# NSA scores of query tiles 2 and 3 from high and low parts in fp32r

## The chip, the cores and the metric

The kernel runs on one NeuronCore of a Trainium2 chip. The metric is the device time of one execution in microseconds (us), the median of several runs. TensorE (PE) multiplies, VectorE (DVE) and ScalarE (ACT) work elementwise, GpSimd (POOL) works elementwise and issues indirect DMAs, SyncE (SP) issues most of the weight DMAs. PEld is TensorE's weight load.

## The reference, cut to what matters

Two transformer blocks run one after the other on 512 tokens of width 1024, in float32. The change lies in the first block, in the Native Sparse Attention (NSA): 8 heads of 64 columns in 2 key/value groups of 4 heads. It has three branches, of which two are touched, the local window of 256 tokens and the selected blocks (with top-8 of 8 blocks this is full causal attention):

```python
lg = jnp.einsum('bqghd,bgqkjd->bqghkj', q_c, k_sel).astype(jnp.float32) * scale + bias_s
p_sel = masked_softmax(lg, mask_s[:, :, :, None], (-2, -1))
o_sel = jnp.einsum('bqghkj,bgqkjd->bqghd', p_sel, v_sel.astype(jnp.float32))
...
lg = jnp.einsum('bqghd,bkgd->bqghk', q_c, kw_c).astype(jnp.float32) * scale + bias_w
p_win = masked_softmax(lg, mask_w[:, None, None, :], -1)
o_win = jnp.einsum('bqghk,bkgd->bqghd', p_win, vw_c.astype(jnp.float32))
out = g_c[..., 0:1] * o_cmp + g_c[..., 1:2] * o_sel + g_c[..., 2:3] * o_win
```

The change is about the two products of q and k (`lg`).

## The kernel before, in words

Everything is written per engine, each engine's program in its own order, joined by semaphores. Large projections are computed as three fp32r products from parts: a value is a high part (its copy rounded to fp32r) plus a low part (the value less the high part), and high x high + high x low + low x high are added up in PSUM (`products`, L2130 is its matmul helper). For each weight tile ACT makes the high part (L948), POOL the low part (L807), through two buffers `w_split`; the raw tiles come through a ring of four (`ring`, loaded by SP at L691 once POOL's low part of the tile four before is made).

`h_split`, the parts of the normed input, lies at `h_base`. It is last read by the token-major projection `vtok`, which ends right before the window attention, and is written again only in the memory attention much later.

An attention of this kernel (`attend` on PE, on DVE, and `softmax` on ACT) runs over 32 units, a unit being one head of one tile of 128 queries; 8 units for each of the query tiles t = 0 to 3. Units come in pairs: of the two heads of a pair one belongs to group 0 (partitions 0 to 63 of `qk`) and one to group 1 (partitions 64 to 127). A unit has 1, 2, 3, 3 blocks of 128 keys in the window attention (t = 0 to 3) and 1, 2, 3, 4 in the selected one. In each turn of the loop PE does, for pair n: the scores of pair n (L2230), then the product with the values of the first unit of pair n-2 (L2255), the transposes of the first unit of pair n-1 (L2245), and the same two for the second units. DVE adds the bias and takes the least (L1545) right after the scores, ACT makes the exponential (L966), PE transposes it, ACT copies the transpose out of PSUM (L983), and PE multiplies it with the values. At pair 6 of the window attention (and each fourth one after) DVE also writes out a finished query tile (L1514 to L1523; at pair 6 the gates too, L1615 to L1617).

The scores are float32 products with 64 rows of contraction. Each appears in the trace as two weight loads and two matmuls.

What stands around the window attention on POOL: the low part of the first `w_out` weight tile before pair 1 and of the second at pair 4 (L807); then nothing until 275.7 us. These two tiles are first read at 265 us, after both attentions. ACT makes their high parts at 158.7 and 165.8 us.

## Time and profile before

| | us |
|---|---|
| median of 3 runs | 2499.2 (2498.59 to 2503.46) |
| the profiled execution, its own time | 2500.74 |
| its span, first to last instruction | 2498.7 |
| PE busy | 2454.7 (98%) |
| PE weight loads busy | 2074.6 (83%) |
| DVE, POOL, ACT busy | 1578.5, 1289.3, 965.6 |
| window attention, scores of t = 2 and 3 (8 pairs) | 174.28 to 196.94 |
| selected attention, scores of t = 2 and 3 (8 pairs) | 228.90 to 253.70 |

PE is busy nearly all the time. Its matmuls are pipelined and overlap in the records (a matmul has about 0.2 us from its start to its end besides what it streams), so how fast PE works is read from the distance between the starts of instructions, not from their durations. "issue" behind an idle time says that the engine waited for nothing that the profile shows.

### The profile page before, as it was taken

The page shows a single profiled execution, that of the slowest core. Times are in us where ns is not written, and L with a number is a line of the kernel's source. Part 1 is how long each engine was busy: PE and PEld are TensorE (multiplying, and loading weights), DVE is VectorE, ACT ScalarE, POOL GpSimd, SP SyncE. Part 2 cuts the span into 40 slices and gives each one's busy share as a digit, 9 for nine tenths or more (in the row PEclk, how much of TensorE's full clock was granted, in tenths as well). Part 3 has the DMA queues.
Part 4 walks back from the last instruction along what each step waited for, and adds up shares of the span by engine and source line. Part 5 has one row for each costly group of instructions (what it writes and reads, how often), then busy time and mean ns, then how long its engine had stood idle before and what let it go on. Part 6 is the DMA issues. An engine that isn't in the chain of part 4 may idle for free.

```text
span 2498.7 us, 32840 instructions
## 1 busy us (share of the span) xinstructions
PE 2454.7 (98%) x12363; PEld 2074.6 (83%) x12363; DVE 1578.5 (63%) x2572; ACT 965.6 (39%) x1573; POOL 1289.3 (52%) x671
## 2 busy tenths in 40 slices
PE   9999999999999999999999999999999999999998
PEld 6877766877786777788789999999999888888886
DVE  2246244776402735422379897998940699999995
ACT  3256455222323435523333333434333433333333
POOL 3630322444454433144434887766666567666662
PEclk9999999999999999999999999999999999999999
DMA  5320222655433221022223888999998899999992
GB/s 215 118 68 1 68 68 76 202 197 182 152 101 127 76 85 66 32 98 93 101 81 118 297 298 287 356 354 360 358 322 260 296 363 359 364 367 361 367 363 90
DMA packets 212733, 508.90 MB, mean 204 GB/s; under 512 B 18401, under 2 KB 101345, under 8 KB 212193
## 3 DMA queue, kind: packets, MB, share of 16 engines
q1 hardware_dynamic: 123696, 338.22, 38.6%
q0 software_dynamic: 36864, 134.23, 15.1%
q10 hardware_dynamic: 52016, 34.36, 4.4%
q8 instruction: 99, 1.62, 0.3%
q14 instruction: 58, 0.47, 0.1%
HBM read 454.31 MB, written 52.43 MB: 203 GB/s over the span
## 4 chain that ended last, share of the span: by engine, by line
PE 89%; DVE 3%; POOL 3%; ACT 3%; DMA 1%; issue 1%; ACTq 0%; DVEq 0%; SPq 0%
PE bank L2130 73%; PE bank L2682 3%; PE bank_and L2130 3%; POOL weight_split L807 3%; PE bank L2255 3%; PE bank_and L2098 2%; PE bank L2245 1%; ACT weight_split L948 1%; PE bank_and L2230 1%; DMA ring<-weights 1%; PE bank L2230 1%; PE bank L2109 1%; PE bank_and L2495 0%; PE bank L2554 0%; DVE h_split L1424 0%
## 5 line engine op out<-in xcount | busy, mean ns | idle before, releaser
L2130 PE MATMUL bank<-h_split,weight_split 128*128 128x384 f32 (+1 forms) x5568 | 1133.9, 362 | 12.9 <-POOL weight_split L807 4.9
L2130 PEld LDWEIGHTS bank<-h_split,weight_split 128*128 128x128 f32 x5568 | 994.7, 188 | 126.1 <-POOL weight_split L807 11.9
L807 POOL TENSOR_TENSOR weight_split<-ring,weight_split 128x1024 fp32r<-128x1024 f32 x182 | 452.9, 2488 | 758.4 <-ACT weight_split L948 758.2
L2130 PE MATMUL bank<-late_weight_split,weighted_split 128*128 128x512 f32 x2268 | 514.8, 389 | 0.0
L2130 PEld LDWEIGHTS bank<-late_weight_split,weighted_split 128*128 128x128 f32 x2268 | 425.5, 188 | 88.3
L834 POOL DMA_INDIRECT arena<-weights,arena x256 | 314.2, 1228 | 146.1 <-DVE arena L1884 59.6
L823 POOL TENSOR_TENSOR weight_split<-ring,weight_split 128x1024 fp32r<-128x1024 f32 x129 | 310.3, 2406 | 120.8 <-ACT weight_split L1321 120.1
L948 ACT ACTIVATE weight_split<-ring 128x1024 fp32r<-128x1024 f32 x182 | 192.0, 1055 | 292.2 <-PE bank L2130 276.9
L1321 ACT ACTIVATE weight_split<-ring 128x1024 fp32r<-128x1024 f32 x130 | 137.8, 1061 | 390.2 <-PE bank L2130 336.3
L2026 DVE TENSOR_TENSOR arena<-arena 128x384 f32<-128x384 f32 x128 | 224.8, 1756 | 21.3 <-DMA arena<-expert_acts 20.9
L823 POOL TENSOR_TENSOR late_weight_split<-ring,late_weight_split 128x1024 fp32r<-128x1024 f32 x63 | 152.7, 2424 | 102.8 <-ACT late_weight_split L1321 102.2
L1884 DVE CUSTOM_DVE_ANT_0 arena<-arena,bank_and 128x1024 f32<-128x1024 f32 x128 | 153.1, 1219 | 49.6 <-DMA arena<-weights,arena 48.7
L1355 ACT ACTIVATE weighted_split<-arena 128x384 fp32r<-128x384 f32 x128 | 67.4, 527 | 270.4 <-DVE arena L2026 261.2
L2016 DVE SCALAR_TENSOR_TENSOR bank_and<-arena,bank_and 128x1024 f32<-128x1024 f32 x127 | 162.6, 1280 | 0.9
L1321 ACT ACTIVATE late_weight_split<-ring 128x1024 fp32r<-128x1024 f32 x126 | 132.8, 1054 | 46.4 <-PE bank L2130 40.5
L2130 PE MATMUL bank<-hidden_layer_split,weight_split 128*128 128x512 f32 x528 | 122.3, 392 | 1.3 <-POOL weight_split L807 1.0
L2130 PEld LDWEIGHTS bank<-hidden_layer_split,weight_split 128*128 128x128 f32 x528 | 98.3, 188 | 24.9 <-issue 2.6
L1486 DVE SCALAR_TENSOR_TENSOR arena<-bank,rstd 128x512 f32<-128x512 f32 x42 | 29.0, 691 | 126.2 <-PE bank L2130 118.0
L2032 DVE TENSOR_TENSOR weighted_split<-arena,weighted_split 128x384 fp32r<-128x384 f32 x128 | 76.2, 596 | 47.0 <-ACT weighted_split L1355 47.0
L2682 PE MATMUL bank<-arena 128*128 128x128 f32 x768 | 93.4, 275 | 0.0
L2682 PEld LDWEIGHTS bank<-arena 128*128 128x128 f32 x768 | 92.3, 192 | 0.0
L2255 PEld LDWEIGHTS bank<-arena 128*128 128x128 f32 x528 | 67.4, 191 | 24.3 <-ACT arena L983 15.8
(349 smaller groups left out, 2718.3 us busy)
## 6 DMA issues: line engine op xcount, KB each, us to landing
ring<-weights SPq DMA_DIRECT2D x493, 512.0 KB
expert_acts<-arena SPq DMA_DIRECT2D x128, 192.0 KB
gates_spread<-arena ACTq DMA_DIRECT2D x24, 1024.0 KB
arena<-gates_spread SPq DMA_DIRECT2D x96, 256.0 KB
arena<-expert_acts SPq DMA_DIRECT2D x128, 192.0 KB
arena<-weights,arena POOLq DMA_INDIRECT x256
arena<-bias_sel ACTq DMA_DIRECT2D x1, 2048.0 KB, 7.8
arena<-bias_band ACTq DMA_DIRECT2D x1, 2048.0 KB, 7.8
```

What stands on the lines that cost most here:

```text
L807: nc.gpsimd.tensor_tensor(w_split[:, (count - 1) % 2, 1, :], ring[:, n % RING, :], w_split[:, (count - 1) % 2, 0, :], ALU.subtract).then_i ...
L823: nc.gpsimd.tensor_tensor(w[:, 1, :], ring[:, (BEFORE + e) % RING, :], w[:, 0, :], ALU.subtract).then_inc(w_lo_ready, 1)
L834: nc.gpsimd.indirect_dma_start(gathered_rows[:, j % GR, :], None, expert_rows, bass.IndirectOffsetOnAxis(ap=pick, axis=0)).then_inc(gather ...
L948: a.activation(w_split[:, s % 2, 0, :], ring[:, n % RING, :], ACT.Copy).then_inc(w_high, 1)
L1321: a.activation(split_of(e)[:, 0, :], ring[:, n % RING, :], ACT.Copy).then_inc(w_hi_ready, 1)
L1884: v.tensor_tensor_reduce(rows_, rows_, wide[:, :], 1.0, 0.0, ALU.mult, ALU.add, dots[:, j:j + 1]).then_inc(gather_used, 1)
L2016: v.scalar_tensor_tensor(out=wide[:, :], in0=rows_, scalar=coef[:, j:j + 1], in1=wide[:, :], op0=ALU.mult, op1=ALU.add).then_inc(gather_us ...
L2026: v.tensor_tensor(weighed[:, e % 2, :], act_in[:, e % AS, :], gblk[:, b % 2, :, j], ALU.mult).then_inc(weighed_ready, 1)
L2032: v.tensor_tensor(p_split[:, e % PS, 1, :], weighed[:, e % 2, :], p_split[:, e % PS, 0, :], ALU.subtract).then_inc(p_lo_ready, 1)
L2130: ins = mm(*args, start=start, stop=stop)
L2255: last = mm(bank[4 + g % 2][:, h * HD:(h + 1) * HD], probT[:, u % 2, c * P:(c + 1) * P], vals(i, c), start=(c == 0), stop=(c == blocks(i) ...
L2682: mm(bank[2 + n % 3][:, (t % 4) * P:(t % 4 + 1) * P], hot1[:, t % HOT, :], hot2[:, t % HOT, :], start=True, stop=True).then_inc(hot_used, 1)
```

## The change

For query tiles 2 and 3 of both attentions the float32 score product is replaced by two fp32r products that are added up in PSUM:

- the first contracts over 128 rows: the stationary operand is `q_split`, which holds in one half of the partitions the high part of a head's queries and in the other half the low part; the moving one is `k_twice`, the high part of the keys in both halves;
- the second (`score_rest`) contracts over 64 rows: the high part of q with `k_low`.

PE does the first products of both units of a pair, then the second ones. The parts lie over `h_split`. POOL makes the high parts of keys and queries and the low parts of the keys in `attention_parts`, which stands in its program ahead of the low part of the first `w_out` tile; nearly every instruction there is followed by a wait for itself. DVE copies the keys' high part into the other half of the partitions at pair 2 (branch 1, window) and pair 9 (branch 0, selected), and makes the queries' low parts, two at each of pairs 3 to 6. PE waits for all of it before the scores of tiles 2 and 3.

```diff
+        q_split = split("late_queries_split", h_base, 0, NH, 2 * P)
+        k_twice = split("keys_high_twice", h_base, 2048, 2, 2, T)
+        k_low = split("keys_low", h_base, 4096, 2, T)
...
+            def key_parts(branch):
+
+                for g in range(2):
+                    nc.gpsimd.tensor_copy(k_twice[half[g], branch, g, :], qk[half[g], 6 + branch, :]).then_inc(k_high, 1)
+                    pool.wait_ge(k_high, 2 * (1 - branch) + g + 1)
+                for g in range(2):
+                    nc.gpsimd.tensor_tensor(k_low[half[g], branch, :], qk[half[g], 6 + branch, :],
+                                            k_twice[half[g], branch, g, :], ALU.subtract).then_inc(k_lowered, 1)
+                    pool.wait_ge(k_lowered, 2 * (1 - branch) + g + 1)
+
+            def attention_parts():
+
+                pool.wait_ge(*taken(first["qk"] + 7))
+                pool.wait_ge(proj_done, first["vtok"] + NT)
+                key_parts(1)
+                for n in range(NH):
+                    g, m = n % 2, n // 2
+                    nc.gpsimd.tensor_copy(q_split[half[g], m + 4 * g, :], qk[half[g], m, 2 * P:T]).then_inc(q_high, 1)
+                    pool.wait_ge(q_high, n + 1)
+                key_parts(0)
...
+                if count == tile_of[first["w_out"]]:
+                    attention_parts()
                 count += 1
                 pool.wait_ge(w_high, count)
...
-            attend(U_WIN, 32, NH, win_blocks, win_bias, lambda i: i // NH * NH + nsa_unit(i)[1], window_out)
+            def key_in_other_half(branch):
+
+                dve.wait_ge(k_high, 2 * (1 - branch) + 2)
+                for g in range(2):
+                    v.tensor_copy(k_twice[half[1 - g], branch, g, :], k_twice[half[g], branch, g, :]).then_inc(k_copied, 1)
+
+            def query_low(n):
+
+                g, m = n % 2, n // 2
+                dve.wait_ge(q_high, n + 1)
+                v.tensor_tensor(q_split[half[1 - g], m + 4 * g, :], qk[half[g], m, 2 * P:T],
+                                q_split[half[g], m + 4 * g, :], ALU.subtract).then_inc(q_low, 1)
+
+            def attention_parts(pair):
+
+                if pair == 2:
+                    key_in_other_half(1)
+                if 3 <= pair < 7:
+                    query_low(2 * pair - 6)
+                    query_low(2 * pair - 5)
+                if pair == 9:
+                    key_in_other_half(0)
+
+            attend(U_WIN, 32, NH, win_blocks, win_bias, lambda i: i // NH * NH + nsa_unit(i)[1], window_out,
+                   after=attention_parts)
...
+            def score_rest(u, w, q, k):
+                mm(bank[S_BANK[u % 4]][:, 0:w], q, k, start=False, stop=True).then_inc(qk_done, 1)
...
+                def scores(pair):
+
+                    both = [i for i in (2 * pair, 2 * pair + 1) if i >= begun]
+                    for i in both:
+                        score(u0 + i, P * blocks(i), q(i), k(i), last=rest(i) is None)
+                    for i in both:
+                        if rest(i):
+                            score_rest(u0 + i, P * blocks(i), *rest(i))
...
+                if t >= 2:
+                    return q_split[:, h, (t - 2) * P:(t - 1) * P]
                 return qk[g * HD:(g + 1) * HD, h % 4, t * P:(t + 1) * P]
...
+                if t >= 2:
+                    if branch:
+                        pe.wait_ge(q_low, min(i % (2 * NH) + 1, NH))
+                    pe.wait_ge(k_copied, 2 * (2 - branch))
+                    pe.wait_ge(k_lowered, 2 * (2 - branch))
+                    return k_twice[:, branch, g, lo * P:(t + 1) * P]
                 return qk[g * HD:(g + 1) * HD, 6 + branch, lo * P:(t + 1) * P]
+
+            def nsa_rest(i, branch, lo):
+                t, h = nsa_unit(i)
+                rows_ = slice(h // 4 * HD, h // 4 * HD + HD)
+                if t >= 2:
+                    return q_split[rows_, h, (t - 2) * P:(t - 1) * P], k_low[rows_, branch, lo * P:(t + 1) * P]
```

## Rows read from the trace of the kernel before

**Rows 1.** The page: the chain that ended last, by engine.
```profile
PE 89%; DVE 3%; POOL 3%; ACT 3%; DMA 1%; issue 1%; ACTq 0%; DVEq 0%; SPq 0%
```

**Rows 2.** Windows: length, busy PE, PEld, DVE, ACT, POOL (us), clock, DMA.
```profile
174.28:196.94 22.66, 22.56 (x167) 16.84 (x167) 10.71 (x42) 17.01 (x52) 0.00 (x0) 1.00 0.00 1
...
228.90:253.70 24.80, 24.80 (x182) 18.41 (x182) 15.64 (x45) 20.40 (x59) 0.00 (x0) 1.00 0.01 1
```

**Rows 3.** PE's timeline, window attention, one pair of 384 keys (start, length, what).
```profile
185.26 0.92 PE L2230 MATMUL bank<-arena 64*128 64x384 f32 x4
186.10 0.88 PE L2255 MATMUL bank<-arena 128*128 128x64 f32 x6
186.82 0.50 PE L2245 MATMUL bank<-const,arena 128*128 128x128 f32 x3
187.16 0.78 PE L2255 MATMUL bank<-arena 128*128 128x64 f32 x6
187.78 0.50 PE L2245 MATMUL bank<-const,arena 128*128 128x128 f32 x3
188.20 0.59 PE L2230 MATMUL bank_and<-arena 64*128 64x384 f32 x2
```

**Rows 4.** PE's timeline, selected attention, a pair of 512 keys.
```profile
249.92 1.13 PE L2230 MATMUL bank_and<-arena 64*128 64x512 f32 x4
250.97 1.10 PE L2255 MATMUL bank<-arena 128*128 128x64 f32 x8
```

**Rows 5.** Weight loads of the scores and the fp32r matmuls, and fp32r matmuls.
```profile
L2230 PEld LDWEIGHTS bank<-arena 64*128 64x128 f32 x112 | 8.4, 184 | 7.6 <-issue 5.0 <-DVE arena L1486 1.2 <-DVE arena L1545 1.1
...
L2130 PEld LDWEIGHTS bank<-late_weight_split,weighted_split 128*128 128x128 f32 x2268 | 425.5, 188 | 88.3
...
L2130 PE MATMUL bank<-late_weight_split,weighted_split 128*128 128x512 f32 x2268 | 514.8, 389 | 0.0
...
151.77 2.56 PE L2130 MATMUL bank<-weight_split,h_split 128*128 128x408 f32 x13
```

**Rows 6.** PE's timeline, end of vtok, and pair 8 of the window attention.
```profile
160.57 0.53 PE L2130 MATMUL bank<-weight_split,h_split 128*128 128x408 f32 x2
...
175.79 0.39 PE L2245 MATMUL bank<-const,arena 128*128 128x128 f32 x2
```

**Rows 7.** POOL: one-input and two-input forms by line, and its timeline.
```profile
L772 POOL TENSOR_SCALAR arena<-arena 128x1024 f32<-128x1024 f32 x8 | 22.6, 2820 | 0.0
L786 POOL TENSOR_TENSOR arena<-arena,sq 128x512 f32<-128x512 f32 x5 | 6.5, 1300 | 9.9 <-ACT sq L869 9.9
...
166.97 2.36 POOL L807 TENSOR_TENSOR weight_split<-ring,weight_split 128x1024 fp32r<-128x1024 f32 x1 [4.73 <-ACT weight_split L948]
```

**Rows 8.** The timelines of DVE and of POOL at 108 and 276 us.
```profile
108.15 2.50 DVE L1592 TENSOR_SCALAR arena<-arena,small 128x512 f32<-128x512 f32 x1
...
107.91 2.46 POOL L807 TENSOR_TENSOR weight_split<-ring,weight_split 128x1024 fp32r<-128x1024 f32 x1 [1.24 <-ACT weight_split L948]
...
275.96 2.42 DVE L1427 TENSOR_TENSOR mem_split<-rms,mem_split 128x256 fp32r<-128x256 f32 x1 [1.52 <-ACT mem_split L916]
...
278.82 0.42 DVE L1427 TENSOR_TENSOR mem_split<-full,mem_split 128x256 fp32r<-128x256 f32 x1
```

**Rows 9.** DVE's timeline, window attention, pairs 3, 6, 7 and 10.
```profile
165.59 0.29 DVE L1545 CUSTOM_DVE_ANT_0 arena<-bank_and,arena 128x128 f32<-128x128 f32 x1 [0.68 <-PE bank_and L2230]
...
170.87 0.42 DVE L1545 CUSTOM_DVE_ANT_0 arena<-bank,arena 128x256 f32<-128x256 f32 x1 [0.85 <-PE bank L2230]
...
173.91 0.41 DVE L1545 CUSTOM_DVE_ANT_0 arena<-bank_and,arena 128x256 f32<-128x256 f32 x1
...
180.31 0.56 DVE L1545 CUSTOM_DVE_ANT_0 arena<-bank,arena 128x384 f32<-128x384 f32 x1 [1.45 <-PE bank L2230]
```

**Rows 10.** ACT's timeline, the exponentials of the first units of pairs 7 and 10.
```profile
174.37 0.51 ACT L966 ACTIVATE arena<-arena 128x256 f32<-128x256 f32 x1 [1.40 <-DVE arena L1545]
...
180.91 0.62 ACT L966 ACTIVATE arena<-arena 128x384 f32<-128x384 f32 x1 [0.44 <-DVE arena L1545]
```

More of the change, by code:

```diff
@@ L786, in add_square @@
                 nc.gpsimd.tensor_tensor(sum_, before, sq[:, n % 2, :], ALU.add).then_inc(sq_summed, 1)
+            half = [slice(g * HD, (g + 1) * HD) for g in range(2)]
+            def key_parts(branch):
[15 more added lines that the diff above has]
+                key_parts(0)
             def add_chunks(n, y):
@@ L2225, in token_major, with score @@
                     release(1)
[L2227 removed]
+            def score(u, w, q, k, last=True):
                 if u >= 4:
                     pe.wait_ge(logits_ready, u - 3)
[L2230 to L2237 removed]
+                ins = mm(bank[S_BANK[u % 4]][:, 0:w], q, k, start=True, stop=last)
+                if last:
+                    ins.then_inc(qk_done, 1)
+            def score_rest(u, w, q, k):
+                mm(bank[S_BANK[u % 4]][:, 0:w], q, k, start=False, stop=True).then_inc(qk_done, 1)
+            def attend(u0, g0, units, per, q, k, blocks, head, vals, before_turn=None, begun=0, busy=(0, 0),
+                       after_turn=None, rest=lambda i: None):
+                def scores(pair):
[5 more added lines that the diff above has]
+                            score_rest(u0 + i, P * blocks(i), *rest(i))
                 def turn_prob(i):
@@ L2266, in attend @@
                     if pair < units // 2:
-                        scores(2 * pair)
-                        scores(2 * pair + 1)
+                        scores(pair)
                     if pair == 1 and before_turn and not after_turn:
@@ L2382, in _ @@
                    lambda i, c: nsa_v(i, 1, first_near(i) + c),
-                   before_turn=lambda: pe.wait_ge(*taken(first["vtok"] + 3)), begun=2, busy=(0, 2))
+                   before_turn=lambda: pe.wait_ge(*taken(first["vtok"] + 3)), begun=2, busy=(0, 2),
+                   rest=lambda i: nsa_rest(i, 1, first_near(i)))
             pe.wait_ge(logits_ready, U_SEL)
@@ L2412, in _ @@
             attend(U_SEL, G_SEL, 32, NH, nsa_q, lambda i: nsa_k(i, 0, 0), causal_blocks, nsa_head,
-                   lambda i, c: nsa_v(i, 0, c), busy=(4, 0))
+                   lambda i, c: nsa_v(i, 0, c), busy=(4, 0), rest=lambda i: nsa_rest(i, 0, 0))
             def turn_merged():
```

12 lines of the change are left out of this document (6 added, 6 removed).

## The prediction

> **What bounds the kernel now.** I read the chain that ended last first: 89% of it is PE [rows 1]. So the question is what PE's time becomes in the two stretches that the change touches, the scores of query tiles 2 and 3. The windows there show PE busy for 22.56 of 22.66 us and for 24.80 of 24.80 us, with the clock at its full 1.00 (2.4 GHz); ACT is the next with 17.01 and 20.40, then DVE with 10.71 and 15.64, and POOL does nothing [rows 2]. These stretches go at PE's pace. Everything that PE saves in them arrives at the end, and what DVE and POOL do besides costs nothing as long as it makes PE wait for nothing.
>
> PE's timeline gives the pace of one pair. With 384 keys the pair's period is 2.94 us (185.26 to 188.20), of which the scores take 0.84 until the products with the values start [rows 3]. They cost a bit more than that: the three transposes ahead of them take 0.42 us until the scores start, against 0.34 where value products follow, and the value products right behind them take 0.72 against 0.62 for the same six a little later. So a pair's scores cost 0.84 + 0.08 + 0.10 = 1.02 us. With 512 keys it is 1.05 [rows 4] + 0.18 = 1.23. The step of 0.21 us for 128 keys says what part of it is streaming: 3 x 0.21 = 0.63 of the 1.02. The other 0.39 is fixed. Four matmuls (two for each unit) fit into 0.63 us because the two units use different halves of the array's rows ("64*128" in the row) and run side by side. This is what the change gives up in its first product.
>
> **PE's part.** Removed: in 16 pairs (8 window pairs with 384 keys, 4 selected ones with 384, 4 with 512) the four float32 matmuls. Added: two fp32r matmuls over all 128 rows, one after the other, and two fp32r ones over 64 rows each. A full fp32r matmul of 512 columns takes 514.8 / 2268 = 0.227 us from start to start; at 408 columns 13 of them end after 2.56 us, which is 0.185 each once the last one's own 0.35 us of length is taken as overlap [rows 5]. The slope is 0.40 ns a column, so 384 columns take 0.175. The first products cost 2 x 0.175 = 0.35 us, or 0.45 with 512. They have the shape of the transposes before them, so I charge them no change of shape. The second products keep the fixed 0.39, since the array goes from full to halved rows and back as it does now, and they stream once, side by side: 0.16 (384 columns at 0.41 ns), or 0.21. Sum: 0.35 + 0.39 + 0.16 = 0.90 against 1.02, and 0.45 + 0.39 + 0.21 = 1.05 against 1.23. PE saves 12 x 0.12 + 4 x 0.18 = 2.2 us.
>
> The trace has no fp32r matmul on 64 rows, so this has two ends. If two of them do not run side by side, a second streaming is added: 12 x 0.16 + 4 x 0.21 = 2.8, and PE loses 0.6 us. If the weight load that is now exposed ahead of the scores hides under the streaming of the first product, each pair saves one more load, 0.11 to 0.12 us by the spacing of the value products (six in 0.72 us) [rows 3], and the gain is 2.2 + 16 x 0.11 = 4.0. I take 2.2, because the score's load stands exposed now although matmuls stream before it too.
>
> Weight loads could also get shorter with the type. The rows say 184 ns for the float32 scores and 188 ns for the fp32r products [rows 5], so I take no gain. The Trainium skill (TensorE: Matmul & The Clock Gate, section Weight-path perf modes) says that a fast weight load is on when there are 128 weights and the input type is not FP32. By that rule fp32r would load faster, and the exposed loads would give about 1.5 us more; the trace does not agree, and nothing below uses it.
>
> The added waits on PE (the low queries, the copied and the lowered keys) are for things done long before: the last low query is made behind DVE's pair 6, and the first score of tile 2 is PE's pair 8; the selected branch's keys are ready some 30 us before it starts. I charge nothing; a wait that is already met sits in PE's queue ahead of the array, as the present ones do in a stretch with 0.1 us of idle time.
>
> **POOL's part.** Its new work starts when vtok's last matmul is done, at 161.1 [rows 6], and nobody else wants POOL until then but the low parts of two w_out tiles. A two-input operation of 512 columns takes 1.30, a one-input one of 1024 columns 2.82 [rows 7], so 1.41 for 512 and 0.71 for 256 at most. The lower end is half a two-input operation, 0.65 and 0.33. A copy is nearest to the one-input row; I take 1.1 and 0.6, and 0.1 for each wait on itself. Then: keys' high parts of the window branch done at 163.5, their low parts at 166.3, the eight queries at 171.9, the selected branch's four operations at 177.1, then w_out's two low parts (2.36 each [rows 7]) at 179.5 and 181.9. Behind these waits in POOL's queue stand only the w_out tiles, 17 us later than now. They are read at 265, so this is hidden by 83 us. The two ring loads on SP's queue that they release move from 162 and 169 to about 180 and 182, where DMA is idle; nothing reads those tiles before 265 either.
> The Trainium skill (GPSIMD Engine Reference, section Performance versus the Vector engine) gives 769 ns for 512 elements in its best case. By that POOL would be done with the queries about 2.5 us earlier, and DVE's part below would come out near 0.5 us in place of 1.3. No row here shows a copy on POOL.
>
> **DVE's part.** This is what can cost. DVE gets two copies at pair 2, two low queries at each of pairs 3 to 6, two copies at pair 9. Alone, a low query has the price of the 256-column form, 0.42 us [rows 8]; a copy 0.28 (the one-input operation at 108.15 ended at 110.65, 0.28 after POOL's at 110.37). But those rows also show that the two engines exclude each other: that operation stood 2.50 us because POOL's of 2.46 had started first, and a two-input one of 256 columns took 2.42 beside a POOL operation against 0.42 without. So each of the ten new operations on DVE up to pair 6 can wait for one POOL operation, 0.6 to 1.3 us, while its biased logits, which read PSUM, do not show this.
>
> What is late next is the exponential of pair 7. DVE's pair 7 starts at 173.91 with no idle time ahead of it, because tile 0 is written out right before [rows 9]; the two low queries of pair 6 stand in its way with their whole 0.84 us. To this come their own waits for POOL (0 to 1.4) and what is carried from pairs 3 to 5, where 0.68 to 1.26 us of idle time per pair meets 0.84 of work and waits (0 to 1.9 carried). Pair 7 is late by 0.84 to 4.1 us. The slack: its exponential ends at 174.37 + 0.51 = 174.88 [rows 10], PE's transpose starts at 175.79 [rows 6], 0.9 us later. So PE stands 0 to 3.2 us; with half of the waits and of the carry, 0.84 + 0.5 + 0.9 - 0.9 = 1.3. At pair 9 the two copies can each meet a w_out tile on POOL: 2 x 2.36 + 0.56 = 5.3 us, against 1.45 of idle time before pair 10 [rows 9] and 2.35 of slack (exponential over at 181.53 [rows 10], transpose at 186.82 - 2.94 = 183.88 [rows 3]): 0 to 1.5, and I take 0.3, as it needs a poor meeting twice. What hides DVE's other new work is that idle time; without it all ten operations would count, 3.9 us.
>
> **The sum.** -2.2 + 1.3 + 0.3 = -0.6 us. On the profiled execution, 2500.74 in all with a span of 2498.7, this gives 2500.1 with a span of 2498.1. The median of the runs stood 1.5 below that execution, so 2498.6. A difference of 0.2%, 5 us, is about what a measurement of this kernel can tell from none.
>
> **The rivals.** First, DVE falls behind (slower than before). Place: DVE between 165 and 176, and at pair 9. Price: up to 3.2 + 1.5 - 2.2 = +2.5, 2501.7. It makes the kernel slower from the point at which pair 7 is late by more than 0.9 + 2.2 = 3.1 us. For it speaks the mutual exclusion [rows 8] and that DVE must follow POOL's pace (0.7 us a query, 1.4 a pair); against it that PE's pairs there are 1.6 to 2.1 us apart and POOL has a head start. Second, the second products do not run side by side: PE loses 0.6, and with 1.6 on DVE the time is 2501.4. Against it: the halves of the array do this now in float32. Third, both at once: +0.6 + 3.2 + 1.5 = +5.3, 2504.5. Fourth, the first product hides the load: 4.0 - 0.6 = -3.4, 2495.8. Nothing in the trace shows a load hidden at that change of shape. That the change doesn't do what it says would need the float32 form to stay; the types are plain in the code, so this has no chance of its own.
>
> **How the numbers follow.** The forecast, 2497.3 to 2500, has 0.45; DVE behind 0.27; no side by side 0.10; both 0.04; the hidden load 0.08; and 0.06 stays for what I have not seen (halved clock where PE stands, for one), half to each side. The best end is 2495.2 (4.0 gained, nothing lost), the worst 2504.5. For 8 in 10 I take 2495.6 to 2503.3. Slower by over 0.2%, above 2504.2: the 0.04, and 0.04 of the rest. Faster by over 0.2%, below 2494.2: 0.05. In between 0.87.
>
> **What would show it.** In the profile after, a pair of 384 keys in tile 3 of the window attention should have a period of 2.82 and one of 512 keys should be 0.18 shorter; the two matmuls of 64 rows should start within 0.01 us of each other, and the first products 0.175 apart. POOL's last query should be ready near 172, its copies 1.1 and 0.6. DVE's low queries should stand between 0.42 and 1.1 us, and pair 7's logits start near 176. The start of tile 2's scores, 174.28 now, should move to about 175.6, and the start of the selected attention to about the same time as now. The prediction is wrong if the periods don't shrink, if tile 2's scores start past 177.5, or if something outside 160 to 260 us moves by more than a microsecond.

## The result

| | before | after |
|---|---|---|
| median of the runs, us | 2499.85 (2498.59 to 2504.38) | 2512.90 (2510.78 to 2534.72) |
| ratio after / before | | 1.0067 [1.0051, 1.0084] |
| profiled execution, us | 2500.74 | 2520.74 |
| its span, us | 2498.7 | 2518.9 |

The prediction was 2498.6 with a range of 2495.6 to 2503.3, and gave "slower by over 0.2%" 8 in 100. The change made the kernel slower, by 13.05 us between the medians (0.52%) and by 0.67% over all runs of both. The measured median lies outside the range. The five runs of after lie 24 us apart, those of before 5.8. That spread belongs to the result, as is shown below. The times below are of the profiled executions, where after is 20.2 us longer than before; between the medians it is 13.

The page of after: the granted clock in 40 slices of 63 us, and the chain that ended last.

```profile
PEclk9997999999999999999999999999999999999999
...
PE 88%; DVE 3%; POOL 3%; ACT 3%; DMA 1%; issue 1%; SPq 0%; ACTq 0%; DVEq 0%
```

The chain is that of before [rows 1]: PE still sets the pace. What is new is the fourth digit of the clock. The stage of the change, cut at the point where it goes wrong (from:to and length, then busy PE, PEld, DVE, ACT, POOL with their counts, granted clock, DMA share, GB/s):

```profile
175.03:181.16 6.13, 0.96 (x8) 0.46 (x6) 5.93 (x13) 0.92 (x4) 3.05 (x2) 0.72 0.55 171
181.16:217.00 35.84, 35.84 (x160) 30.46 (x161) 10.45 (x38) 17.35 (x49) 0.00 (x0) 0.52 0.00 1
...
249.06:272.70 23.64, 23.64 (x182) 19.47 (x180) 15.81 (x46) 20.37 (x58) 0.00 (x0) 1.00 0.01 2
```

Read the first two rows. In 6.13 us PE does 0.96 us of work while DVE is busy for 5.93. Then PE is busy all the time, but at a granted clock of 0.52. Finer cuts put the fall to 0.5 (1.2 GHz) at 177.7 and the return to 1.00 (2.4 GHz) at 215.2, so 37.5 us at half. The last row is the selected attention: it is at full clock, all PE, and shorter than before (23.64 us against 24.80 in [rows 2]; the cuts are at the same two pairs).

PE's timeline around the stop (start, length, line, operation, tiles, shape, count, idle time ahead):

```profile
175.03 0.59 PE L2289 MATMUL bank<-keys_high_twice,late_queries_split 128*128 128x384 f32 x2
175.55 0.44 PE L2294 MATMUL bank<-keys_low,late_queries_split 64*128 64x384 f32 x2
181.16 1.11 PE L2324 MATMUL bank<-arena 128*128 128x64 f32 x4 [5.17 <-ACT arena L1016]
...
183.53 0.99 PE L2289 MATMUL bank_and<-keys_high_twice,late_queries_split 128*128 128x384 f32 x2
```

The ledger follows from the starts of the pairs. Pair 8 starts 0.75 us late (175.03 against 174.28). Pair 9 starts 6.66 late (183.53 against 176.87): the stop of 5.17, and a first stretch at half clock. The selected attention starts 20.34 late (233.92 against 213.58), so 13.7 more, lost at the half clock, where a pair of 384 keys takes 5.18 us instead of 2.95. Its last pair starts 19.16 late (269.08 against 249.92), so the selected attention gives 1.18 back. **In this execution about 6 us are a stop (0.75 + 5.17) and about 15 us are the clock. The second is an estimate: PE works for 34.0 of the 37.5 us, and a pair takes 5.18 there instead of 2.82. About 2 us are gained.** What is left to the end of the span, another 1.0 us, comes mostly from steps of 1.4 to 1.7 us up and down between 320 and 520 us. They are taken up at the end of this document.

Who makes PE stop? PE waits at the value products of pair 6 (181.16), which need ACT's copy of pair 6's transposes. That copy stands in ACT's program behind the exponential of pair 7, and this waits for DVE's logits of pair 7. DVE's timeline:

```profile
172.93 0.47 DVE L1648 TENSOR_SCALAR arena<-arena 128x96 f32<-128x96 f32 x1
173.44 0.75 DVE L1649 RECIPROCAL arena<-arena 128x96 f32<-128x96 f32 x1
174.23 1.59 DVE L1650 TENSOR_SCALAR arena<-arena,const 128x8 f32<-128x8 f32 x1
175.85 0.20 DVE L1547 RECIPROCAL arena<-arena 128x8 f32<-128x8 f32 x1
176.09 2.02 DVE L1553 TENSOR_TENSOR arena<-arena 128x8 f32<-128x8 f32 x1
178.14 0.69 DVE L1556 TENSOR_TENSOR arena<-bank,arena 128x512 f32<-128x512 f32 x1
178.87 0.87 DVE L1665 TENSOR_TENSOR late_queries_split<-arena,late_queries_split 64x256 fp32r<-64x256 f32 x2
179.77 0.42 DVE L1578 CUSTOM_DVE_ANT_0 arena<-bank_and,arena 128x256 f32<-128x256 f32 x1
```

This is the write-out of query tile 0, and behind it the two low queries of pair 6. Two operations on 8 numbers per partition take 1.59 and 2.02 us; before they took 0.23 and 0.17. The first one, on 96, takes 0.47 instead of 0.21. Pair 7's logits start at 179.77 instead of 173.91 [rows 9]. These 5.86 us are: pair 6 begun 1.37 late (172.24 against 170.87), 3.47 more in the three operations, 0.87 for the low queries, and 0.15 between them. And POOL's timeline:

```profile
161.05 1.28 POOL L801 CAST keys_high_twice<-arena 64x512 fp32r<-64x512 f32 x2 [7.53 <-PE bank L2189]
...
165.08 4.01 POOL L815 CAST late_queries_split<-arena 64x256 fp32r<-64x256 f32 x8
169.16 1.36 POOL L801 CAST keys_high_twice<-arena 64x512 fp32r<-64x512 f32 x2
170.60 2.74 POOL L804 TENSOR_TENSOR keys_low<-arena,keys_high_twice 64x512 fp32r<-64x512 f32 x2
173.42 4.67 POOL L840 TENSOR_TENSOR weight_split<-ring,weight_split 128x1024 fp32r<-128x1024 f32 x2
```

The last row holds the low parts of the two w_out tiles. Before, the second of them started at 166.97 [rows 7] and the first at 159.86. Queued behind the new work, they now run from 173.42 to 178.09. DVE's 1.59 ends at 175.81, 0.03 us behind the first of the two (175.79); DVE's 2.02 ends at 178.11, 0.03 us behind the second (178.08). This is the mutual exclusion of [rows 8], which the prediction knew of and charged to the wrong instructions.

**Theory A**, made from these traces: (1) the displaced low parts of w_out keep DVE out of tile 0's write-out and so stop PE; (2) the stop lets TensorE's clock fall to half, and this attention does not bring it back, for up to tens of microseconds; (3) the new scores are quicker on PE as predicted. Rivals: the lateness is that of the ten new operations on DVE (B); the clock falls because of the new scores and not because of the stop (C); the loss lies in the time that PE's new form itself takes. The expectations below from stall_filled_less on use other letters: there "Theory D" is A, the stall together with what the clock does after it, "C2" is C, and "Theory E" is the second half of part 2.

### The profile page after: what moved, and what is told of

It reads as the page before. It is cut to its first block, busy times and chain, and to the rows that moved or that the text cites. A ratio compares the mean times of both kernels' runs of the same rounds, so it can differ in the third digit from the quotient of the medians.

```text
span 2518.9 us, 32918 instructions
## 1 busy us (share of the span) xinstructions
PE 2465.7 (98%) x12363; PEld 2087.2 (83%) x12363; DVE 1582.7 (63%) x2584; ACT 965.7 (38%) x1573; POOL 1297.0 (51%) x687
## 4 chain that ended last, share of the span: by engine, by line
PE 88%; DVE 3%; POOL 3%; ACT 3%; DMA 1%; issue 1%; SPq 0%; ACTq 0%; DVEq 0%
PE bank L2189 71%; PE bank L2765 3%; PE bank_and L2189 3%; PE bank L2324 3%; POOL weight_split L840 3%; PE bank_and L2157 2%; PE bank L2314 1%; ACT weight_split L981 1%; DMA ring<-weights 1%; PE bank L2168 1%; PE bank_and L2289 1%; PE bank L2289 1%; PE bank L2637 0%; PE bank_and L2578 0%; DVE h_split L1457 0%
## 5 line engine op out<-in xcount | busy, mean ns | idle before, releaser
L867 POOL DMA_INDIRECT arena<-weights,arena x256 | 307.4, 1201 | 147.1 <-DVE arena L1943 59.8
L2324 PEld LDWEIGHTS bank<-arena 128*128 128x128 f32 x528 | 75.4, 211 | 25.0 <-ACT arena L1016 15.7
L2765 PEld LDWEIGHTS bank<-arena 128*128 128x128 f32 x768 | 92.3, 192 | 0.0
```

Of the source, the lines that this page charges most:

```text
L867: nc.gpsimd.indirect_dma_start(gathered_rows[:, j % GR, :], None, expert_rows, bass.IndirectOffsetOnAxis(ap=pick, axis=0)).then_inc(gather ...
L2324: last = mm(bank[4 + g % 2][:, h * HD:(h + 1) * HD], probT[:, u % 2, c * P:(c + 1) * P], vals(i, c), start=(c == 0), stop=(c == blocks(i) ...
L2765: mm(bank[2 + n % 3][:, (t % 4) * P:(t % 4 + 1) * P], hot1[:, t % HOT, :], hot2[:, t % HOT, :], start=True, stop=True).then_inc(hot_used, 1)
```

## The experiments

The medians of the kernel before beside these runs were 2500.66 to 2500.91.

**1. Hold the low parts of w_out back** until tile 1 is written out, so that they can't meet tile 0.

```diff
                 if count == tile_of[first["w_out"]]:
                     attention_parts()
+                    pool.wait_ge(head_out, 2)
```

> The change, with one wait more: POOL holds the low parts of the first two w_out tiles back until DVE has written out tile 1 of the window attention (head_out 2, about 183 us). Theory A (collision): in the changed kernel these two operations of 2.36 us came at 173.4 and 175.7, just when DVE wrote out tile 0 (small SBUF operations of 1.59 and 2.02 us in place of 0.23 and 0.17), so PE stood 5.2 us and its clock fell to half for 37.5 us. Then here DVE's pair 7 is about 1.5 us late, PE stands under 1.5 us, the clock stays at 1.00 in 160 to 220 us, and the time is that of before less 0.5 to 2 us (ratio 0.999 to 1.000). Theory B (own work): DVE's ten new operations alone make PE stand; then PE still stands 3 us or more and the time stays 5 us or more above that of before. Theory C (the new products or waits on PE lower the clock): the clock halves here as well and the time stays near 2511.

Measured: 2515.85 (2508.39 to 2526.53), ratio 1.0068 [1.0041, 1.0094]; the profiled span was 2507.8. DVE in the same place, and the window behind the stop:

```profile
174.51 0.23 DVE L1651 TENSOR_SCALAR arena<-arena,const 128x8 f32<-128x8 f32 x1
175.02 0.17 DVE L1554 TENSOR_TENSOR arena<-arena 128x8 f32<-128x8 f32 x1
175.94 0.87 DVE L1666 TENSOR_TENSOR late_queries_split<-arena,late_queries_split 64x256 fp32r<-64x256 f32 x2
176.85 0.42 DVE L1579 CUSTOM_DVE_ANT_0 arena<-bank_and,arena 128x256 f32<-128x256 f32 x1
```

```profile
179.63:194.00 14.37, 14.37 (x76) 11.76 (x75) 5.68 (x20) 7.80 (x23) 4.68 (x2) 0.64 0.17 49
```

Part 1 of A holds: both operations are back at 0.23 and 0.17, pair 7's logits come 2.9 us earlier than in after, and PE's stop shrinks from 5.17 to 1.95 us. But the time is no better, because B holds too: the two low queries of pair 6 (0.87 us) and what came before them still leave a stop of 1.95, and the clock still fell, here for 10.2 us. My expectation of a clock that stays at 1.00 was missed. All six runs took 2508.4 or more, at a mean granted clock of 0.987 to 0.995, against 0.995 to 0.998 for the 18 of before. So the length of the stop is not the price; the clock is.

**2. The displacement alone**, in the kernel before: hold the same low parts until tile 0's value products are done.

```diff
+                if count == tile_of[first["w_out"]]:
+                    pool.wait_ge(pv_done, NH)
                 count += 1
```

> The kernel before, with one wait more: POOL's low part of the first w_out tile waits for the values of tile 0 (pv_done 8), so both low parts fall on DVE's write-out of tile 0, as in the changed kernel; nothing else is changed. Theory A: DVE's small operations there take 1.5 to 2.4 us, pair 7 of DVE is 3 to 4 us late, PE stands 2 to 4 us; the time rises by 2 to 4 us, and by 10 to 20 if the clock falls as well. Theories B and C: no change (ratio 1.000), since neither DVE's new work nor PE's new products are there.

Measured: 2504.59 (2502.12 to 2520.35, 10 runs), ratio 1.0024 [1.0007, 1.0040].

```profile
170.02 4.68 POOL L809 TENSOR_TENSOR weight_split<-ring,weight_split 128x1024 fp32r<-128x1024 f32 x2 [16.34 <-PE bank L2257]
...
173.27 1.46 DVE L1619 TENSOR_SCALAR arena<-arena,const 128x8 f32<-128x8 f32 x1
...
175.81 0.41 DVE L1547 CUSTOM_DVE_ANT_0 arena<-bank_and,arena 128x256 f32<-128x256 f32 x1
```

With none of the new arithmetic, moving these two operations stretches an 8-element operation from 0.23 to 1.46 us, the one on 96 from 0.21 to 0.93, and puts pair 7's logits 1.9 us late (3 to 4 were expected). PE stopped for 2.04 us, and the selected attention started 1.9 late. In the profiled execution the clock stayed at 1.00 in this stage. Its mean was still 0.995, because of short stretches at half clock elsewhere, such as the kernel before has too; so a mean of 0.995 alone tells nothing. Three of the ten runs had a lower one (0.991 to 0.994), with 2509.4, 2512.9 and 2520.4 us. So displacement alone costs about 4 us between the medians, and the clock falls after a stop of this size in some runs only.

**3 and 4. Fill the stop with matmuls.** PE runs full-array float32 products of constants ahead of pair 8 and writes them to the bank that pair 8's scores then overwrite; nothing else is changed in after. If the clock is the price, a kernel that does more useless work on PE must be faster.

```diff
                     both = [i for i in (2 * pair, 2 * pair + 1) if i >= begun]
+                    if u0 == U_WIN and pair == 8:
+                        pe.wait_ge(logits_ready, 13)
+                        keep_busy(11, 0)
```

> The change, with 11 matmuls of 512 columns on constants (4.7 us) on PE ahead of the scores of pair 8 of the window attention, into the bank that these scores then overwrite: the time in which PE stood is filled, the collision stays. Theory A with the clock as a second part: the clock stays at 1.00, pair 9 starts near 182, the time is 2 to 5 us above that of before (the stall of 5 us less 2 us of gain). If the clock falls because of the new products (theory C) or for another cause, it is at half in 178 to 215 us as before and the time stays 10 us or more above.

Measured: 2508.73 (2507.71 to 2510.38), ratio 1.0031 [1.0018, 1.0044]. I had mis-sized the filling: a float32 product runs as two matmuls, and eleven calls took 9.5 us, so pair 8 started at 184.35. Even with this, the time is 4 us better than after (8 us better than after's second measurement beside these runs), the mean clock was 0.996 to 0.998 in every run, and the spread fell from 24 to 2.7 us. The right size, `keep_busy(6, 0)`, 5.2 us:

> The change with 6 float32 fill products of 512 columns ahead of pair 8's scores (each is two matmuls of 0.43 us, so 5.2 us), not 11, which made 9.5 us and pushed pair 8 to 184.35. Theory D (the loss is the stall plus what the clock does after it): the clock stays at 1.00 and the time is that of before plus the filled 5.2 us, less 2.2 us of gain, so +3 to +4.5 us (ratio 1.0012 to 1.0018), with a spread of runs as small as that of before. If the fill does not reach far enough, some runs fall to half clock and lie 10 us or more above.

Measured: 2504.66 (2501.88 to 2508.20, 10 runs), ratio 1.0012 [1.0003, 1.0021].

```profile
172.30:182.50 10.20, 9.64 (x45) 5.59 (x44) 9.01 (x20) 3.91 (x15) 5.68 (x3) 1.00 0.32 103
182.50:218.60 36.10, 35.07 (x249) 28.39 (x247) 21.86 (x63) 19.59 (x56) 0.00 (x0) 1.00 0.01 1
```

The second row stands against 35.84 us at 0.52 in after. Pair 9 starts 5.7 us late (182.54; 6.7 in after) and the clock stays at 1.00; the selected attention starts at 218.58 instead of 233.92. C falls: the new scores alone don't lower the clock.

**5. The change again**, unaltered, beside these runs.

> The changed kernel, unchanged, for a second profile on the same chip as the others. All theories: ratio near 1.005 to 1.007. Theory A: again PE stands about 5 us between 176 and 181 us; how long the clock stays at half may differ from the first profile, since its five runs lie between 2510.8 and 2534.7.

Measured: 2516.45 (2508.89 to 2532.51), ratio 1.0070 [1.0036, 1.0105]. PE's stop is 5.16 us, that of the first profile of after to a hundredth, but the half clock lasts 17.1 us here, not 37.5:

```profile
183.60:196.00 12.40, 12.40 (x59) 10.11 (x57) 4.95 (x17) 5.81 (x18) 0.00 (x0) 0.56 0.01 2
```

This is the spread of the runs: the stop is the same every time, its after-effect isn't. Over the runs, a mean clock of 0.995 goes with spans near 2509, 0.990 with 2519 and 0.984 with 2533.

**6. Hold and fill**: experiment 1 with `keep_busy(3, 0)` ahead of pair 8.

> The change with the two w_out low parts held until tile 1 is written out, and 3 fill products (2.6 us) ahead of pair 8's scores. Without the fill PE still stood 1.95 us behind pair 8 and the clock fell in every run (10.2 us at half in the profile, more in others). Theory D: with the fill the clock stays at 1.00 in all runs, time before -0.5 to +2 us. Rival C2 (the new form of the scores makes the clock fall, with or without a stall): half clock in 180 to 220 us again, 7 us or more above before.

Measured: 2505.26 (2503.05 to 2506.71), ratio 1.0013 [1.0003, 1.0022], clock 0.995 to 0.997. The clock is held and the tail is gone, but the filling costs what the stop did: pair 8 at 177.44, the selected attention at 215.96. The median is 4.4 us above before, where I expected at most 2.

**7. Spread the new work**: both holds on POOL (the selected branch's key parts after tile 0's write-out, w_out's low parts after tile 1's), and no low query ahead of pair 7.

```diff
+                pool.wait_ge(head_out, 1)
                 key_parts(0)
...
                     attention_parts()
+                    pool.wait_ge(head_out, 2)
...
-                if 3 <= pair < 7:
-                    query_low(2 * pair - 6)
-                    query_low(2 * pair - 5)
+                if pair in (3, 4, 5, 8):
+                    n = (3, 4, 5, 8).index(pair)
+                    query_low(2 * n)
+                    query_low(2 * n + 1)
```

> The change with its work on POOL and VectorE put elsewhere: POOL makes the selected branch's key parts only after tile 0 is written out, and the w_out lows after tile 1; DVE makes the last two low queries at pair 8 and none at pair 6, and the others at pairs 3 to 5. No fill on PE. Theory D: DVE's pair 7 is under 0.9 us late, PE stands under 0.6 us anywhere between 165 and 200, the clock stays at 1.00, and the time is 1 to 2.5 us under before (ratio 0.9990 to 0.9996). Rival C2: the clock falls all the same, ratio over 1.002.

Measured: 2503.18 (2499.20 to 2506.61, 11 runs), ratio 1.0006 [0.9997, 1.0015]; span 2498.8, clock 0.997.

```profile
173.41 0.17 DVE L1555 TENSOR_TENSOR arena<-arena 128x8 f32<-128x8 f32 x1
174.22 0.42 DVE L1580 CUSTOM_DVE_ANT_0 arena<-bank_and,arena 128x256 f32<-128x256 f32 x1
174.44 1.28 POOL L801 CAST keys_high_twice<-arena 64x512 fp32r<-64x512 f32 x2 [5.27 <-DVE arena L1558]
...
183.00 4.70 POOL L842 TENSOR_TENSOR weight_split<-ring,weight_split 128x1024 fp32r<-128x1024 f32 x2 [4.52 <-issue]
```

```profile
174.30:197.00 22.70, 22.20 (x173) 18.45 (x171) 14.18 (x47) 17.25 (x54) 8.52 (x6) 1.00 0.15 48
```

Pair 7's logits start 0.3 us after those of before, PE's longest stop there is 0.30, pair 8 starts at 174.32 (174.28 before), and the clock stays at 1.00. The loss of 13 us is gone but for 2.3 us between the medians, which is within the noise, with the same arithmetic on all engines; it was the order of the work. The last selected pair starts at 248.50 against 249.92: 1.4 us gained. At the end of the span the gain isn't there, so my expectation of 1 to 2.5 us below before was missed. Two slips of 1.9 and 1.6 us, near 430 and 512 us in the feed-forward stage, eat it in this execution.

**8. Experiment 1 with the scores still in float32** (w_out's low parts are held as there; all parts are made, none is used by a score), to see whether the fall needs the new scores.

```diff
-                if t >= 2:
+                if t >= NT:
```

(in the function that picks the rest; the two that pick queries and keys lose their branch for tiles 2 and 3)

> As lows_held (parts made by POOL and DVE, w_out lows held back), but PE computes the scores in float32 from qk as the kernel before, and the parts are not used. Same work on POOL and DVE, so the same late pair 7. Theory D alone (the stall of 1.95 us is what makes the clock fall): half clock in most runs, time +5 to +20 us, like lows_held. Rival C2: with the float32 scores the clock falls rarely, as in the kernel before with late lows (stall 2.04 us, 6 of 10 runs at a clock of 0.996 or more), and the time is +2 to +4 us, which would put part of the loss on the new form of the scores.

Measured: 2509.44 (2503.76 to 2519.06, 10 runs), ratio 1.0032 [1.0017, 1.0047].

```profile
179.58:198.80 19.22, 19.22 (x85) 13.88 (x84) 6.00 (x21) 9.05 (x25) 4.66 (x2) 0.56 0.17 56
```

PE stopped for 1.84 us and the clock fell to half for 17.1 us with float32 scores. By mean clock and time it fell in seven of ten runs (0.991 to 0.995, 2508.3 us and more); the other three took 2503.8 to 2504.2 at 0.997. With the new scores and a stop of 1.95 it fell in six of six. So the stop is enough without the new scores, and C falls from this side too. Whether the new scores make the fall more likely can't be told from six and ten runs.

**9. The kernel before again**, for the slips.

> The kernel before, unchanged, for a second profile. In parts_spread the scores' stretches were over 1.4 us sooner than in the one profile of before, but 1.6 and 1.7 us of that were lost again in two steps near 430 and 512 us, in the feed-forward stage, which the change doesn't touch; the same steps stand in nearly every other run's profile. If they are chance of the one profile of before, this profile shows them too, against the first: the distance between 260 and 900 us is then 1.5 to 3 us longer than in the first. If they come from the change, it is not.

Measured: 2500.59, span 2498.5. The pairs have the same periods to a hundredth. A slip of 1.4 us near 512 us shows here too, against the first profile of the same kernel, and none near 430. Of the 13 other profiles 12 have the slip near 512, so there the first profile of before was the lucky one.

**10. Experiment 7 with float32 scores**, to weigh the new form against the old one with all other work equal.

> As parts_spread, with PE's scores in float32 from qk as the kernel before; the parts are made and not used. Against parts_spread this gives what the new form of the scores is worth with nothing else in the way. By the prediction's sum: 2.2 us slower than parts_spread, so 2505.4 if that is at 2503.2, ratio 1.0012 to 1.0018 against before; the pairs of 384 keys have a period of 2.95 in place of 2.82 and the last one of 512 has 3.82 in place of 3.66. If the gain is none, the two are equal.

Measured: 2502.10 (2498.66 to 2505.99, 11 runs), ratio 1.0002 [0.9993, 1.0012]. The selected attention in this kernel and in experiment 7:

```profile
229.00:253.90 24.90, 24.90 (x184) 18.45 (x182) 15.71 (x45) 20.47 (x59) 0.00 (x0) 1.00 0.01 1
```

```profile
228.40:252.20 23.80, 23.80 (x183) 19.62 (x182) 15.86 (x47) 20.51 (x58) 0.00 (x0) 1.00 0.01 2
```

In the traces the last selected pair starts at 250.09 here and at 248.50 there: 1.6 us for the new scores, where 2.2 was expected. At 440 us the two kernels are level again: experiment 7 has slipped by 1.9 near 430, this one by 0.2. In the medians there is nothing of it (1.1 us the other way, each interval some 2 us to either side). My expectation of a kernel that is slower by it was missed.

**11. Undo only the holds of experiment 7** (both of them, on POOL), keeping its order on DVE.

> As parts_spread (low queries at pairs 3, 4, 5 and 8), but POOL holds nothing back, so both w_out low parts again run from about 173.3 to 178 us, on DVE's write-out of tile 0. Theory D: DVE's small operations there take 1.5 to 2.4 us again, PE stands 3 to 5 us behind pair 8, the clock falls in most runs, the time is 8 us or more above before. If DVE's own two low queries at pair 6 had been the cause, there would be no stall here and the time would be that of parts_spread.

Measured: 2515.90 (2512.34 to 2521.37), ratio 1.0051 [1.0036, 1.0067].

```profile
174.19 1.58 DVE L1650 TENSOR_SCALAR arena<-arena,const 128x8 f32<-128x8 f32 x1
...
176.05 2.02 DVE L1553 TENSOR_TENSOR arena<-arena 128x8 f32<-128x8 f32 x1
...
178.71 0.41 DVE L1578 CUSTOM_DVE_ANT_0 arena<-bank_and,arena 128x256 f32<-128x256 f32 x1
```

```profile
182.46:211.00 28.54, 28.54 (x131) 23.92 (x129) 8.82 (x32) 13.24 (x37) 0.00 (x0) 0.53 0.00 1
```

The collision is back with 1.58 and 2.02, PE stops for 4.14 us, and the clock is at half for 30.7. B alone would have left this kernel near experiment 7; it costs some 13 us more. Of the stop of 5.17 us, taking POOL's part away (experiment 1) removes 3.2, taking DVE's low queries at pair 6 away (here) removes 1.0; so POOL's order is the larger cause.

**12. Call the clock back**: after, with five filling calls (ten matmuls) ahead of pair 9, when the stop is over and the clock has fallen.

```diff
+                    if u0 == U_WIN and pair == 9:
+                        pe.wait_ge(logits_ready, 15)
+                        keep_busy(5, 6)
```

> The change as it is, stall and all, with 5 fill products of 512 columns (4.3 us at full clock, 8.6 at half) on PE ahead of the scores of pair 9, behind the stall. Theory E: the clock falls at about 178 and stays down because this attention's own pattern does not bring it back, while dense fill does; then the stretch at half clock ends by about 195 in every run, the slow tail (2520 and more) is gone, and the median is 2507 to 2512 with a spread under 4 us. If the clock's return has nothing to do with what PE does, the spread stays at 10 to 20 us.

Measured: 2512.67 (2512.01 to 2513.44), ratio 1.0042 [1.0027, 1.0058]; span 2511.6.

```profile
181.00:184.80 3.80, 3.51 (x14) 3.00 (x15) 0.63 (x4) 2.95 (x10) 0.00 (x0) 0.50 0.01 2
184.80:188.20 3.40, 3.40 (x11) 1.49 (x9) 0.00 (x0) 0.00 (x0) 0.00 (x0) 1.00 0.00 0
188.20:214.00 25.80, 25.80 (x207) 22.40 (x205) 12.48 (x43) 15.48 (x45) 0.00 (x0) 1.00 0.01 2
```

The stop (5.14 us) and the fall are those of after. The clock comes back within the filling, 1.0 us after its first product, after 6.8 us at half instead of 37.5 and 17.1, and stays at 1.00 for the attention behind it. The median is that of after (0.7 above the range that I expected), since the filling costs what it saves, but the runs lie 1.4 us apart instead of 24. One profile alone could be chance, as the half clock also ended by itself after 10.2 us in experiment 1; the narrow spread of all four runs says that it isn't. So part 2 of A stands: products of this kind bring the clock back, and the attention's own stream did not for up to 37.5 us.

## Why the prediction was wrong, step by step

**PE's part was right in kind, and a third too large.** The pairs of the selected attention have periods shorter by 0.12 (384 keys) and 0.16 to 0.18 (512). One pair of 384 keys in after, at full clock:

```profile
253.33 0.50 PE L2314 MATMUL bank<-const,arena 128*128 128x128 f32 x3
253.58 0.59 PE L2289 MATMUL bank<-keys_high_twice,late_queries_split 128*128 128x384 f32 x2
254.10 0.45 PE L2294 MATMUL bank<-keys_low,late_queries_split 64*128 64x384 f32 x2
254.47 0.88 PE L2324 MATMUL bank<-arena 128*128 128x64 f32 x6
...
256.40 0.60 PE L2289 MATMUL bank_and<-keys_high_twice,late_queries_split 128*128 128x384 f32 x2
```

The period is 2.82, as forecast. From the last transposes to the scores it is 0.25 instead of the 0.42 of [rows 3], so the first product indeed pays no change of shape, and from the scores to the values 0.89 instead of 0.84. The two 64-row products start 3 to 4 ns apart, so they run side by side; the second rival falls, and so does the fourth, the hidden load. The first products start 0.26 apart, not 0.175. Of the 2.2 us of the sum, 1.2 came in the selected attention, and 1.4 to 1.6 in the whole where nothing stood in the way (experiments 7 and 10). The rest is missing on the window side: in experiment 7 only 0.3 of its 0.96 us (8 pairs x 0.12) arrived, PE being busy for 22.20 of 22.70 us there.

**POOL's part was mis-sized, and this mattered.** I took 1.1 and 0.6 us for a copy of 512 and of 256 columns, near the one-input row of [rows 7], because no row showed a copy. They take 0.60 to 0.69 (four in the trace) and 0.39 to 0.48. The lower ends, 0.65 and 0.33, were nearest. The Trainium skill (GPSIMD Engine Reference, section Performance versus the Vector engine) has 769 ns for 512 elements as a best case; the four here take 0.60 to 0.69, less than that, and the measurement decides. The key parts of the selected branch were thus ready at 173.3 and not at 177.1, and the low parts of w_out slid onto tile 0's write-out at 172.9.

**The step that failed is "hidden by 83 us".** For the displaced w_out tiles I asked only who reads them. I didn't ask whom they keep out while they run. The exclusion of [rows 8] was in my hands, with the right durations (2.36 for POOL's operation, 2.50 and 2.42 for DVE's beside it), but I charged it only to the operations that the change adds to DVE, and for the w_out tiles only to the two copies at pair 9. Tile 0's write-out was named in the prediction as what stands ahead of pair 7, and three of its small operations were held by POOL in after, for 0.26, 1.36 and 1.85 us: 3.5 that the sum lacks. The forecast that each low query stands between 0.42 and 1.1 held for seven of eight; one took 1.38. The two copies at pair 9 met nothing (0.88 together) and cost nothing, where 0.3 was charged.

**The slack of 0.9 us was not there.** I took it from the exponential of pair 7 to PE's transposes of pair 7. But ahead of these transposes PE has the value products of pair 6, and they wait for the copy that ACT makes right behind that exponential. Before:

```profile
174.88 0.36 ACT L983 ACTIVATE arena<-bank 128x256 f32<-128x256 f32 x1
...
175.29 0.66 PE L2255 MATMUL bank<-arena 128*128 128x64 f32 x4
```

The copy ends at 175.24 and the first value product starts 0.05 us later. So every delay of pair 7's logits arrives at PE whole: with logits 5.86, 2.94, 1.90 and 0.31 us late (after, experiments 1, 2 and 7), that value product is 5.87, 2.95, 1.90 and 0.31 late. What makes the stops shorter than this is that pair 8 itself starts later (0.75 in after). Without the 0.9 the first rival becomes +3.4, and the sum +0.3.

**The clock was priced at nothing.** "Halved clock where PE stands" had 0.06 together with all else unseen, half to each side. It carried about 15 of the 21 us lost in the profiled execution. The rivals had PE standing for up to 3.2 us, and each should have had the clock as its second half: a stop of 1.84 to 1.95 us was enough in 7 of 10 and in 6 of 6 runs. The first rival, DVE falling behind, was the right mechanism with its price far too low: +2.5 in the text, +13 between the medians and +20 in the profile. The profile of before had no row of a half clock in this stage, but it also had no stop of over a microsecond there. Elsewhere it had such rows, and the prediction made no use of them:

```profile
323.61 6.66 PE L2130 MATMUL bank<-weight_split,mem_split 128*128 128x256 f32 x41 [1.84 <-POOL weight_split L807]
```

```profile
324.60:328.00 3.40, 3.40 (x18) 3.40 (x18) 3.30 (x6) 2.03 (x4) 1.32 (x1) 0.50 0.76 239
...
375.80:379.20 3.40, 3.40 (x9) 2.67 (x8) 1.08 (x1) 1.23 (x2) 0.00 (x0) 0.50 0.00 0
```

Behind a stop of 1.84 us at 323.6, and behind one of 1.90 us at 375.3, the clock was at 0.50. Under the dense projections there it came back after 3.4 us; that it would stay down for tens of microseconds under this attention no row of before could show.

**The signs to look for.** The periods and the side-by-side products came as forecast. A start of tile 2's scores past 177.5 was given as a sign of failure; they started at 175.03, and the damage came one pair later, behind the scores and ahead of the values. That sign watched one step too early: pair 7's logits, forecast for 176, stood at 179.77 and told it.

**Slips in the arithmetic.** Half of pair 6's waits (0 to 1.4) is 0.7 and not 0.5. The fourth rival takes 0.6 for DVE where the sum has 1.6, so it should have been 2496.8. Faster and slower by over 0.2% take 0.04 and 0.05 out of a rest of 0.06. None of them changes the outcome.

**What stays open.** Best order and all (experiment 7), the change is equal to the kernel before within 0.15%, and not shown to beat it. Where its 1.4 to 1.6 us go is only in part settled. Behind 260 us all profiles differ by the same few steps. Some are short half clocks near 324, 376, 795 and 911 us, which come and go from profile to profile, in the two of before too, and cost up to 1.7 us each. Others are slips of 1.4 to 2.1 us near 430 and 476 us, where PE waits for POOL's low part of a weight tile (2.1 us at the longest in experiment 7, 0.7 in the same stretch of before). Eight of the nine profiles with the new scores have one or both of these slips, and none of the five with float32 scores, whether the parts are made or not. So the new scores may well bring them about and pay back their gain there. How they would do so isn't shown, and no run was made for it.

## What to carry to other kernels

When work is added to a queue, what stands behind it moves too: ask of each displaced operation not only who waits for its result, but also whose port or engine it takes while it runs, at both ends of its new place. And take a slack from the first instruction that waits, not from a later one: here a copy stood between the two, and the 0.9 us were none. Where TensorE sets the pace in a light, latency-bound stage, price a stop of some 2 us with a stretch at half clock behind it, not with its own length. Look in the profile of before for half clocks behind stops of that size anywhere in the kernel. A spread of runs that grows from 6 to 24 us is itself a sign of it.

## What the runs showed of the hardware

- **The exclusion of POOL and DVE reaches the smallest operations.** Two operations on 128x8 elements took 2.02 and 1.59 us against 0.17 and 0.23. The reciprocals (0.75 and 0.20) ran on beside POOL's, and so did the biased logits of pair 6, which read PSUM (0.42 each, at 172.24 and 172.59, beside POOL's low keys). The Trainium skill (SBUF — State Buffer, section SBUF: two separate sides) says that of a GpSimd operation and a DVE operation that needs the shared pair of ports, whichever starts first holds it for its whole instruction; by that rule the trace agrees: both DVE operations end 0.03 us behind POOL's.
- **A busy PE did not bring the clock back.** In after, PE is recorded busy for 35.84 of 35.84 us at a granted 0.52, with 128-column transposes, 64-column float32 products and 384-column scores. With ten float32 matmuls of 512 columns on the full array (4.4 us) put behind the stop, it was back 1.0 us after the first of them started. The Trainium skill (TensorE: Matmul & The Clock Gate, section What's actually happening) says that the default is throttled and activity releases it. By that rule the clock should have come back under a PE that was busy throughout; in this stage it stayed at 1.2 GHz for up to 37.5 us, and the measurement decides.
- **At about 2 us the fall comes in some runs only.** After stops of 5.17, 5.16, 5.14, 4.14, 1.95 and 1.84 us in this stage the clock fell in the profiles; after one of 2.04 it didn't. By mean clock and time it fell in six of six runs with 1.95, seven of ten with 1.84 and three of ten with 2.04, so the length alone doesn't order them. In the first two kernels PE also stood for 0.56 us at about 173.5, some 2.5 us ahead of the stop, in the third it didn't; whether that matters wasn't tried. Where nothing called it back, the half clock lasted 10.2 to 37.5 us.
- **fp32r on half the rows.** Two fp32r products on 64 rows run side by side as float32 ones do (starts 3 to 4 ns apart), and an fp32r weight load on 64 rows takes what a float32 one takes (183 against 184 ns).
